# One product of 512 tokens per load of weights in the general projections, and other places in SBUF for the token tiles and the modulation vectors

## What is computed

```python
# first block, layer l (context leaves after the first of two layers)
hx = rmsnorm(x, g_pre) * (1 + scale) + shift       # the same for the context
p  = hx @ w_in[l]                                  # 1024 -> 2816
y  = merge(attention, fourier, conv) @ w_out[l]    # 1024 -> 1024
x  = x + gate * rmsnorm(y, g_post)
# second block, layer l
x = x + 0.5 * m2 * swiglu(ada_norm(x), ffn_w_in[l, 0], ffn_w_out[l, 0])   # 1024 -> 2*2816 -> 1024
x = x + m5 * mixer(ada_norm(x))                    # 1024 -> 3088 or 3104, and 1024 -> 1024
x = x + 0.5 * m8 * swiglu(ada_norm(x), ffn_w_in[l, 1], ffn_w_out[l, 1])
# the context tokens pass through the same, up to the last mixer
return rms_norm(x, final_g)
```

## Time and profile before

| | |
|---|---|
| median of 3 runs | 2312.89 us |
| the runs | 2312.33, 2312.89, 2319.12 us |
| span of the profiled execution, first to last instruction | 2314.2 us |
| mean granted TensorE clock | 0.987 of 2.4 GHz |
| TensorE matmuls (PE) | 2227.1 us busy, 96% of the span, 19320 records |
| TensorE weight loads (PEld) | 2091.2 us busy, 90% |
| VectorE | 1145.4 us, 49% |
| ScalarE | 846.8 us, 37% |
| GpSimd | 176.3 us, 8% |
| DMA | 315.76 MB, mean 136 GB/s |

### The profile page before, as it was taken

How to read it: one execution, slowest core, us unless ns; L and a number is a source line. 1 busy time by engine, 2 the same in 40 slices (tenths; PEclk the granted TensorE clock), 3 DMA queues, 4 the chain that set the end, 5 groups by cost and what they waited for, 6 DMA issues and landing times. The chain is left out here.

```text
span 2314.2 us, 46991 instructions
## 1 busy us (share of the span) xinstructions
PE 2227.1 (96%) x19320; PEld 2091.2 (90%) x19320; DVE 1145.4 (49%) x1930; ACT 846.8 (37%) x1384; POOL 176.3 (8%) x150
## 2 busy tenths in 40 slices
PE   6999999899999999998999999999999999999998
PEld 5986798799999999976999999999999998979998
DVE  5227375653433445456653333454343446487665
ACT  4226454632221233248432222243232234455444
POOL 0003112100000010501200000010000010001000
PEclk9999999999999999999999999999999999999999
DMA  9853544445676244520354666242233233225573
GB/s 297 234 167 86 172 133 104 128 147 154 186 216 186 86 131 117 149 80 28 102 175 141 190 207 189 84 126 85 81 114 94 86 96 101 74 82 146 168 202 112
DMA packets 515900, 315.76 MB, mean 136 GB/s; under 512 B 16035, under 2 KB 513274, under 8 KB 515622
## 3 DMA queue, kind: packets, MB, share of 16 engines
q1 hardware_dynamic: 515160, 313.45, 46.1%
q10 hardware_dynamic: 590, 0.16, 0.0%
HBM read 312.50 MB, written 1.06 MB: 135 GB/s over the span
## 5 line engine op out<-in xcount | busy, mean ns | idle before, releaser
L1118 PE MATMUL ps<-h_hi,w_hi 128*128 128x256 f32 x3376 | 728.0, 280 | 3.5 <-DVE h_lo L1726 1.7
L1118 PE MATMUL ps<-h_lo,w_hi 128*128 128x256 f32 x3376 | 720.6, 278 | 0.0
L1118 PE MATMUL ps<-h_hi,w_lo 128*128 128x256 f32 x3376 | 720.6, 278 | 0.0
L1118 PEld LDWEIGHTS ps<-h_hi,w_hi 128*128 128x128 f32 x3376 | 537.8, 189 | 22.9 <-issue 21.6
L1118 PEld LDWEIGHTS ps<-h_lo,w_hi 128*128 128x128 f32 x3376 | 539.4, 189 | 0.1
L1118 PEld LDWEIGHTS ps<-h_hi,w_lo 128*128 128x128 f32 x3376 | 537.9, 189 | 0.0
L1960 DVE TENSOR_TENSOR w_lo<-stage,w_hi 128x1024 fp32r<-128x1024 f32 x227 | 285.0, 1258 | 441.5 <-ACT w_hi L1467 440.9
L1467 ACT ACTIVATE w_hi<-stage 128x1024 fp32r<-128x1024 f32 x227 | 236.6, 1055 | 334.4 <-PE ps L1118 200.4
L1960 DVE TENSOR_TENSOR w_lo<-deep,w_hi 128x1024 fp32r<-128x1024 f32 x184 | 226.1, 1234 | 226.9 <-ACT w_hi L1467 225.2
L1467 ACT ACTIVATE w_hi<-deep 128x1024 fp32r<-128x1024 f32 x184 | 191.9, 1055 | 179.7 <-PE ps L1118 141.4
L1118 PE MATMUL ps<-g_hi,w_hi 128*128 128x256 f32 x1100 | 232.9, 280 | 0.2
(11 more groups left out here) (413 smaller groups left out, 2858.0 us busy)
## 6 DMA issues: line engine op xcount, KB each, us to landing
modw<-in_ada_w SPq DMA_DIRECT2D x72, 1024.0 KB, 6.7
stage<-in_ffn_w_in SPq DMA_DIRECT2D x88, 512.0 KB, 3.9
deep<-in_ffn_w_in SPq DMA_DIRECT2D x88, 512.0 KB, 3.9
modw<-in_w_mod SPq DMA_DIRECT2D x18, 1024.0 KB, 6.1
stage<-in_w_in SPq DMA_DIRECT2D x30, 512.0 KB, 5.3
stage<-in_ffn_w_out SPq DMA_DIRECT2D x32, 384.0 KB, 3.5
stage<-in_even_w_in SPq DMA_DIRECT2D x24, 512.0 KB, 4.0
deep<-in_ffn_w_out SPq DMA_DIRECT2D x32, 384.0 KB, 3.4
```

What stands on the lines that cost most here:

```text
L1118: last = mm(ps[:, j, v - a:v - a + SEQ], w_part[wp][:, u % RING, c, :], x_part[xp][:, x, v:v + SEQ], start=first and wp == xp and v == a, ...
```

## The change

Two edits. In `chunk` the loop over the tokens in steps of SEQ goes, and one matmul takes all columns of `tok`, 512 or 256. In the table `sizes` the tiles are laid out anew: `modA0` (128 bytes) comes between `big` and `hT`, `svec` (2176 bytes, 128 more than a multiple of 256) moves in front of `stage`, and `modA1` to `modA3` go to the end. With the base of `big` at 0 modulo 256, `hT`, `mixT` and `vtok` now lie at 128, `svec` at 192, `stage`, `scr` and `modw` at 64. So the weight slots are 192 bytes (modulo 256) behind `h_hi` and `h_lo`, where they were 64, and still 64 bytes behind `g_hi` and `g_lo`.

```diff
-        sizes = {"resid": KC * NT, "big": 24 * NT, "hT": KC * NT, "mixT": KC * NT, "vtok": TT * D + TT * ML_HEADS, "stage": STAGE * KC * P,
-                 "scr": 2 * RING * KC * P, "modw": 2 * KC * SEG,
-                 "wfbd": 4 * P, "svec": 2 * KC * 34}
+        sizes = {"resid": KC * NT, "big": 24 * NT, "modA0": 2 * KC * 2, "hT": KC * NT, "mixT": KC * NT, "vtok": TT * D + TT * ML_HEADS,
+                 "svec": 2 * KC * 34, "stage": STAGE * KC * P, "scr": 2 * RING * KC * P, "modw": 2 * KC * SEG, "wfbd": 4 * P, "modA1": 2 * KC * 2,
+                 "modA2": 6 * KC * 2, "modA3": 6 * KC * 2}
...
-        modA = [sb(f"modA{i}", [P, 2 if i < 2 else 6, KC, 2]) for i in range(4)]
+        modA = [over(f"modA{i}", f"modA{i}", 0, [P, 2 if i < 2 else 6, KC, 2]) for i in range(4)]
...
             def chunk(j, u, c, x, first, final):
                 for wp, xp in W_X:
-                    for v in range(a, b, SEQ):
-                        last = mm(ps[:, j, v - a:v - a + SEQ], w_part[wp][:, u % RING, c, :], x_part[xp][:, x, v:v + SEQ],
-                                  start=first and wp == xp and v == a, stop=final and wp == "lo", skip_group_check=True)
+                    last = mm(ps[:, j, 0:b - a], w_part[wp][:, u % RING, c, :], x_part[xp][:, x, a:b],
+                              start=first and wp == xp, stop=final and wp == "lo", skip_group_check=True)
                 return last
```

## The result

The change makes the kernel **0.6% slower**: 2328.58 us (median of 4 runs, 2322.16 to 2330.90) against 2312.61 us (4 runs, 2310.88 to 2319.12) of the kernel before, taken beside it. The ratio is 1.0063, with a 95% interval of 1.0041 to 1.0085. The forecast was 2247 us, and the result lies above the range.

The account below looks back on a forecast made before the run. TensorE, busy 96% of the span, was taken as the bound, its instructions laid end to end. 5,394 x (228.3 - 216) ns = 66 us off 2314.2 gave a 2248 span, median 2247; other costs 0; range 2230 to 2312.

Parts of the forecast that it names:

- I take 216 ns, because the plain records are at the full clock: General products: a float32r matmul of 512 columns costs 216 ns, taken from four plain float32 records of 256 columns.
- the sum: TensorE's row: 5,394 pairs at 228.3 ns become matmuls at 216 ns, 66 us off, all on the path.
- The reason given for the overhead: Weight load and 256-column stream end together, each late by 6.7 or 11.2 ns; 213 ns of stream hides the load whole.
- The formula of the Trainium skill: Distance of matmuls of N columns, N / 2.4 + 2.5 ns: 109.2 for 256, 215.8 for 512; saves 13 us, to 2299.
- the bounds of 14 us less and 13 more: New places, matmuls staying at 256 columns: all at the cheaper price 14 us less, all at the dearer 13 more; 0 taken.
- Overhead per load: Rival, 20%: each load adds 6.7 or 11.2 ns whatever the stream's length; 220.0 or 224.5 ns, 2268 or 2292 us.
- Overhead per column: Rival, 8%: the float32r stream itself is slow, 226.8 ns for 512 columns; 8 us off, 2304.
- Apart by tile: Rival, 10%: 192 bytes suits long streams, 64 does not; `h` wins 49 us, `g` loses 10, 2275.
- Slower: Rival, 12%: long streams locked at 235.8 ns by where stream and load read; 40 us more, 2353; loss from 228.3 ns on.
- the doubled dear form: The dearer of two prices of a 256-column matmul, 117.9 ns, kept per column: 2 x 117.9 = 235.8 ns for 512.
- the feed of weights: General products: a unit of 24 matmuls takes 5.2 us instead of 5.5; the feed carries twice that rate, cost 0.
- the three signs named as proof of an error: Long matmuls 220 ns or more apart; `h` and `g` differing; TensorE beginning to wait for `w_lo`.

## Why the prediction was wrong

**The step that failed** is "I take 216 ns, because the plain records are at the full clock". A float32r matmul of 512 columns took 229.15 ns on `h` and 233.33 on `g`. With these the sum would have been 4,008 x (229.15 - 228.0) + 1,386 x (233.33 - 231.4) = 7 us more, where it had 66 us less: every other factor of it, the 5,394 matmuls and the 228.3 ns of a pair of before (228.9 by the distances), was right. The measured difference is 16 us, of which these 7 are shown to be the long products' and 2.5 the latent ones'. The rows it was taken from could not carry the price. At the half clock the stream asks for a column half as often, and the plain float32 records are of another data type. Both showed that the overhead can be absent; neither showed a float32r stream at full clock.

**The reason given for the overhead** was that load and stream of 256 columns end together and are late for each other, so that a long stream would hide the load whole. The load is hidden whole (PEld 80%, from 90%), yet the loss doubled with the columns, from 6.7 to 13.3 ns at the lowest. Loads of 64 and 32 columns, or of one column repeated, left the streams at 225 to 235 ns. The loss is the stream's own: about 17/16 of the columns' time at the lowest.

**The formula of the Trainium skill** (TensorE: Matmul & The Clock Gate, Back-to-back issue gap), N / 2.4 + 2.5 ns, which that section gives for a single isolated matmul, makes 215.8 of 512 columns. The trace of the change disagrees with it as that of before did for 256. It is met by streams of two columns in turn (215.8 to 216.0), and nearly by streams of one column repeated (215.0 to 216.0).

**The second edit** was priced at 0, "because both forms occur at the present places and nothing in the rows ties a form to a place". The runs tie the time to the layout, since alone it costs 26 us, but not form to place: both forms occur at both places. That cost is nearly all on the short general products, which the first edit abolishes. On what stays short it was small: latent `h` +2.5 us, seams +2.3, token products -2.5, within the bounds of 14 us less and 13 more. The bounds held. That the whole came near 0 is in part luck, since two of the three effects go up and one goes down.

**The rivals.** "Overhead per load", the likeliest of them, had 220.0 or 224.5 ns; it failed with the forecast, since the overhead grew with the columns. "Overhead per column" was the right mechanism, with 226.8 ns, which is about the minimum that the runs show; it lacked the 2.4 to 6.5 ns by place, which turn 8 us less into 7 more. "Apart by tile" was right in its core, that a distance which suits a long stream need not suit a short one, and that `h` at 192 would beat `g` at 64; the difference is 4.2 ns and not 20. "Slower" set its point at 228.3 ns: both tiles are past it, by 0.9 and 5.0 ns, so its sign is right, by another road than the doubled dear form (235.8 ns). The same page of the Trainium skill (Step-by-step) says that load and stream have independent read ports, by which the load would take nothing from the stream. For the length of the load the runs agree in part: no shorter load brought a straight stream below 225 ns, but single streams of the same rows moved by up to 7 ns down and 6 up. And the distance between the two tiles does count, by up to 7 ns in the mean of a row, which that rule has no place for.

**What held:** the records (13,926), the feed of weights, the idle time before the line, the last FFN at 113 to 118 ns. Two of the three signs named as proof of an error came true: distances above 220 ns, and `h` apart from `g`.

## What to carry to other kernels

Take the price of a stream from a row with the same data type, the same clock and the same walk through memory; a floor that shows at half the clock or in another type is only a bound. Two matmuls of 256 float32r columns merged into one of 512 gained nothing here, since the sixteenth goes with the columns and not with the number of instructions. What gained 3% was the order: two columns 1024 bytes apart in turn, with the bank read back in the same turns.

## What was unexpected of the hardware

A float32r stream at 2.4 GHz that walks straight through its columns took about 17/16 of their time at the lowest (113.3, 170 and 226.7 ns for 256, 384 and 512; the lowest mean of one stream in a row of 512 was 225), and up to 8 ns more; for 512 columns the mean of a row goes by the distance of the weights from the tokens modulo 256 bytes. The corrections in bfloat16 fit the same 226.7. Two columns 1024 bytes apart in turn, or one column again and again, took 215 to 216 ns. Closer turns were far worse: 279 ns at 512 bytes, 490 at 256.

Open is how the reads in SBUF bring these numbers about: why 17/16, why 0 and 192 bytes are better than 64 for a long stream, and what sets a whole stretch of short ones to 113.3 or to 117.8 ns at the same place. Not tried: a stream with no load beside it, and the order in turn for the products of 256 columns, which still cost 113 to 118 ns and make up about a quarter of TensorE's time.
